# Gates of the second expert layer: one of four parts kept in the staging buffer, the rest read back four slots at a time

## The reference

```python
idx = jnp.take_along_axis(cidx, pos, axis=-1)
g = jax.nn.softmax(top, axis=-1).astype(h.dtype)
...
def block(args):
    hx, ix, gx = args
    act = jax.nn.gelu(jnp.einsum('td,tkd->tk', hx, u_tab[ix]))
    return jnp.einsum('tk,tkd->td', gx * act, v_tab[ix])
```

## Time and profile before

| | us |
|---|---|
| median of 3 runs | 2998.86 |
| lowest and highest | 2987.83, 3002.03 |
| profiled execution | 3011.89 |
| its span, first to last instruction | 3010.1 |
| its slot loop, first to last `apply` of the second layer | 2241.6 to 2971.1 |

### The profile page before, as it was taken

The page is one execution under the profiler, slowest core; times in us unless marked ns, Lnnn a source line. Parts: engine busy times, 40 slices in busy tenths (PEclk is TensorE's granted clock), DMA queues, the critical chain, the costliest instruction groups (busy, mean ns, idle before and its releaser), DMA issues. The chain is left out here.

```text
span 3010.1 us, 44098 instructions
## 1 busy us (share of the span) xinstructions
PE 2578.7 (86%) x16181; PEld 2269.8 (75%) x16181; DVE 2375.5 (79%) x4626; ACT 1204.6 (40%) x1806; POOL 678.8 (23%) x486
## 2 busy tenths in 40 slices
PE   7976897789999889999879797897779999999765
PEld 4964797788998778887658677796678888888544
DVE  8876689985658999998883565489978888888886
ACT  3344343663333333333334223443654444444322
POOL 0000152111110112213320000152323443434552
PEclk9987899899999999999998898898989999999997
DMA  5720343687678889988861323144889999999995
GB/s 214 280 70 36 122 136 124 240 290 256 231 241 300 301 301 304 315 303 257 270 225 43 127 98 118 54 138 146 297 313 353 358 348 341 349 333 351 323 328 179
DMA packets 333353, 708.38 MB, mean 235 GB/s; under 512 B 172848, under 2 KB 175696, under 8 KB 326368
## 3 DMA queue, kind: packets, MB, share of 16 engines
q1 hardware_dynamic: 272896, 466.60, 45.5%
q0 software_dynamic: 55360, 201.38, 18.5%
q10 hardware_dynamic: 4896, 37.75, 3.1%
HBM read 640.89 MB, written 64.72 MB: 234 GB/s over the span
## 5 line engine op out<-in xcount | busy, mean ns | idle before, releaser
L1998 PE MATMUL pe_s<-hl_hi,pq_uh 128*128 128x320 f32 (+2 forms) x2304 | 719.2, 312 | 47.8 <-DVE pq_ul L163 26.2
L1999 PE MATMUL pe_s<-hl_lo,pq_uh 128*128 128x320 f32 (+2 forms) x2304 | 707.7, 307 | 0.0
L2000 PE MATMUL pe_s<-hl_hi,pq_ul 128*128 128x320 f32 (+2 forms) x2304 | 706.6, 307 | 0.0
L2081 PE MATMUL peer_acc<-val_vh,val_w 128*128 128x512 f32 x2048 | 612.4, 401 | 85.7 <-DVE val_w L163 85.6
L2081 PEld LDWEIGHTS peer_acc<-val_vh,val_w 128*128 128x128 f32 x2048 | 385.1, 193 | 182.3 <-DVE val_vl L163 104.4
L1998 PEld LDWEIGHTS pe_s<-hl_hi,pq_uh 128*128 128x128 f32 x2304 | 452.2, 196 | 70.6 <-issue 37.7
L1999 PEld LDWEIGHTS pe_s<-hl_lo,pq_uh 128*128 128x128 f32 x2304 | 452.6, 196 | 8.4
L2000 PEld LDWEIGHTS pe_s<-hl_hi,pq_ul 128*128 128x128 f32 x2304 | 451.4, 196 | 0.0
L2255 POOL DMA_INDIRECT pe_frow<-in_peer_v,pe_fidx x192 | 317.6, 1654 | 557.4 <-DVE pe_fh L2431 239.4
L2255 POOL DMA_INDIRECT pe_frow<-in_peer_rows,pe_fidx x192 | 236.5, 1232 | 838.5 <-DVE pe_frow L2415 775.1
L163 DVE TENSOR_TENSOR val_vl<-val_vr,val_vh 128x1024 fp32r<-128x1024 f32 x256 | 312.4, 1220 | 108.7 <-ACT val_vh L2199 107.9
(11 more groups left out here) (489 smaller groups left out, 4010.9 us busy)
## 6 DMA issues: line engine op xcount, KB each, us to landing
pq_ur<-in_peer_u SPq DMA_DIRECT2D x256, 512.0 KB
val_vr<-in_peer_v SPq DMA_DIRECT2D x256, 512.0 KB
gates<-gate_stg ACTq DMA_DIRECT2D x30, 1024.0 KB, 8.0
val_mrow<-in_ada_rows SPq DMA_DIRECT2D x56, 512.0 KB
val_gr<-gates SPq DMA_DIRECT2D x128, 160.0 KB, 4.9
pq_ur<-in_w_query SPq DMA_DIRECT2D x32, 512.0 KB, 7.8
s_wv<-val_out SPq DMA_DIRECT2D x32, 512.0 KB
val_gr<-gates SPq DMA_DIRECT2D x128, 128.0 KB
```

The lines of the kernel that those rows point to most:

```text
L1998: pe.matmul(o, r32(uh[:, b, k]), r32(hi[:, k, a:T]), start=k == 0, stop=False)
L1999: pe.matmul(o, r32(uh[:, b, k]), r32(lo[:, k, a:T]), start=False, stop=False)
L2000: mm = pe.matmul(o, r32(ul[:, b, k]), r32(hi[:, k, a:T]), start=False, stop=k == KC - 1)
L2081: mm = pe.matmul(acc[:, 2 * t + c, :], r32(lhs[:, b, w]), r32(rhs[:, b, c * 512:(c + 1) * 512]), start=False, stop=False, skip_group_check ...
```

## The change

`Plan` gets two more numbers: how many of the parts stay in the staging buffer (`held`) and how many slots one gate load covers (`each`). The first layer has 0 and 1, which is what it did; the second has 1 and 4.

```diff
+        self.held, self.each = held, each
+        self.stored = self.parts - held
+        self.odd_stored = (self.parts + 1) // 2 - held
...
-PLANS = Plan(64, [3] * 12 + [2] * 2), Plan(128, [2] * 16)
+PLANS = Plan(64, [3] * 12 + [2] * 2, 0, 1), Plan(128, [2] * 16, 1, 4)
...
-        gr = x.sb("gr", [P, 2, PARTS, HALF])
+        gr = x.sb("gr", [P, 2, plan.stored, EACH * HALF])
...
-            def gate(n, b):
-                src = gates_dram[0:PARTS, :, bass.ds(n, 1), :]
-                sp.dma_start(gr[:, b], src.rearrange("h p a c -> p h (a c)")).then_inc(gload[b], 16)
+            def gate(m):
+                src = gates_dram[0:plan.stored, :, m * EACH:(m + 1) * EACH, :]
+                sp.dma_start(gr[:, m % 2], src.rearrange("h p a c -> p h (a c)")).then_inc(gload[m % 2], 16)
...
                 if n == RING:
-                    sp.wait_ge(gst1, 16 * ((PARTS + 1) // 2))
-                    gate(0, 0)
-                    gate(1, 1)
+                    sp.wait_ge(gst1, 16 * plan.odd_stored)
+                    if plan.held:
+                        sp.wait_ge(gst2, 16 * (PIECES - 1) * plan.odd_stored)
+                    gate(0)
+                    gate(1)
...
-                    sp.wait_ge(applied, z.n + 1)
...
-                    gate(z.n + 2, b)
+                    if (z.n + 1) % EACH == 0 and z.n + 1 + EACH < NB:
+                        sp.wait_ge(applied, z.n + 1)
...
+                        gate((z.n + 1) // EACH + 1)
...
-                if c >= full:
+                if full <= c < plan.stored * (full + 1) + full:
                     store_piece(c, (c - full) // (full + 1), (c - full) % (full + 1))
...
-            act.wait_ge(evacd, CHUNKS)
-            store_rest(PARTS - 1, SOON, SOON + REST)
+            if not plan.held:
+                act.wait_ge(evacd, CHUNKS)
+                store_rest(PARTS - 1, SOON, SOON + REST)
...
             def apply(z, ahead):
-                b = (z.n + ahead) % 2
-                dve.wait_ge(gload[b], z.turn(ahead) * 16 + 16)
-                dve.wait_ge(drained, z.n + (ahead + J + 3))
-                a = A[:, z.place(ahead)]
-                v.tensor_tensor(a, a, gr[:, b].rearrange("p h c -> p (h c)"), ALU.mult).then_inc(applied, 1)
+                n = z.n + ahead
+                m, at = n // EACH, n % EACH * HALF
+                dve.wait_ge(gload[m % 2], m // 2 * 16 + 16)
+                dve.wait_ge(drained, n + (J + 3))
+                a = A[:, z.place(ahead), 0:held].rearrange("p (h c) -> p h c", c=HALF)
+                ins = v.tensor_tensor(a, a, gr[:, m % 2, :, at:at + HALF], ALU.mult)
+                if plan.held:
+                    a = A[:, z.place(ahead), held:TOKENS]
+                    ins = v.tensor_tensor(a, a, stg[:, 1, n], ALU.mult)
+                ins.then_inc(applied, 1)
```

More of the change, by code:

```diff
@@ L1685, with __init__ @@
 class Plan:
-    def __init__(self, fetched, groups):
+    def __init__(self, fetched, groups, held, each):
         self.fetched = self.first = fetched
@@ L1854, in mix_experts @@
     RING, LAST, SPANS, CHUNKS, PARTS = plan.ring, plan.last, plan.spans, plan.chunks, plan.parts
-    FROM, TOKENS = plan.first, plan.tokens
+    FROM, TOKENS, EACH = plan.first, plan.tokens, plan.each
+    held = plan.stored * HALF
     flat = s.sb("A", [P, RING * TOKENS])
@@ L1888, in mix_experts @@
         else:
-            x.sb("kept", [P, 2 * NKEYS * HALF - 6 * D - 2 * TOKENS])
+            x.sb("kept", [P, 2 * NKEYS * HALF - 6 * D - 2 * plan.stored * EACH * HALF])
         pair = x.sb("w", [P, 2, 2 * TOKENS])
@@ L1960, in slot @@
                     value(z.n + 2, b)
-                    sp.wait_ge(applied, z.n + 1)
-                    if z.n + 2 >= SOON:
-                        sp.wait_ge(gst2, 16 * ((PIECES - 1) * ((PARTS + 1) // 2 - 1) + 2))
-                    gate(z.n + 2, b)
+                    if (z.n + 1) % EACH == 0 and z.n + 1 + EACH < NB:
+                        sp.wait_ge(applied, z.n + 1)
+                        if z.n + 2 >= SOON and not plan.held:
+                            sp.wait_ge(gst2, 16 * ((PIECES - 1) * (plan.odd_stored - 1) + 2))
+                        gate((z.n + 1) // EACH + 1)
                 if layer == 0:
@@ L2227, in slot @@
                 expert_gelu(LAST + z.n)
-                if z.n == 0:
+                if z.n == 0 and not plan.held:
                     store_rest(PARTS - 1, SOON + REST, NKEYS)
```

## The result

The changed kernel takes 2980.3 us (median of 13 runs) against 2999.0 of 13 runs of the kernel before on the same chip: ratio 0.9939, 95% interval 0.9925 to 0.9953, 18.6 us less. The forecast of 2962, 37 us less, had the sign, and about twice the size of the first measurement.

What follows compares the result with a forecast made beforehand. PE and the DMA engines were taken as both almost full in the middle, with DVE waiting for gates. Middle 19, tail 12 and entry 8 less 2 for DVE made 37 us, giving 2962 us; range 2938 to 2990.

Steps and rivals of the forecast that it cites:

- Entry: Start of the second layer's slot loop, 2226 to 2304 us: 8 us gained (3 to 12), mainly from stores leaving the holes.
- hole of 9 us: At the entry, DVE waits 9.2 us for slot 2's gates; moving 3 MB of stores out was to return 5.1 us.
- Middle: 80 second-layer slots, 2304 to 2788 us: 19 us gained (8 to 26) from earlier gate loads and freed DMA time.
- the values take the place of the gates: Rival for middle and tail: values land as late as gates did, only 5 us there, 2988 us in all; chance 0.12.
- The full engines: Middle: DMA engines 97% busy, 5.87 us a slot, taken as almost full; 0.25 us a slot freed, to 5.62.
- packet prices: DMA engine time for each packet: 17 ns for 256 bytes, 50 for 1 KB, 176 for 4 KB.
- PE's floor: Middle: PE needs 5.75 us of each 6.05 us slot, so it can return at most its waiting time.
- Tail: 37 last slots without products, 2793 to 2971 us: 12 us gained (5 to 25), less 2 for DVE's split `apply`.
- the sign that I had named for packets and not bytes alone: Tail: with the DMA share unchanged, GB/s staying at 325 means only bytes counted; rising GB/s means packets did.
- The second instruction's price: DVE's `apply` split into 192 and 64 columns: 74 ns a slot with overlap, 2 us lost in the tail (0 to 6).
- Only bytes count: Rival for the whole loop: memory is full, not the engines' packets; 17 us gained, 2982 us; chance 0.16.
- Slower: Rival for the loop: DVE's added instruction and bursts of gate loads cost more than the entry gains; 3032 us; chance 0.06.

Runs made afterwards that it cites:

- e1: The changed kernel, but gates loaded for one slot at a time, the last part still held in the staging buffer; 2977.3 us, ratio 0.9909.
- e4: The changed kernel, but the last part is also stored to DRAM as before (4 MB in three DMAs), which nobody reads; 2988.5 us, ratio 0.9941.
- e2: The kernel before with gates loaded for four slots at a time, all four parts stored in DRAM; 2997.3 us, ratio 0.9975.
- e3: The changed kernel with SP's order in a second-layer slot turned: value block, gates, then table block; 2944.0 us, ratio 0.9795.
- e6: The kernel before with only SP's second-layer order turned (value block, gates, then table block); 2968.8 us, ratio 0.986.
- e7: The changed kernel with gates loaded one slot at a time and SP's second-layer order turned (values, gates, table block); 2950.5 us, ratio 0.981.
- e9: The same kernel as e3, run again on another chip; 2941.5 us, ratio 0.980 to the kernel before.
- e10: The same kernel as e9 with two more unused DVE multiplications in each second-layer slot; 2948.6 us, ratio 0.9816.

## Why the prediction was wrong

**Entry: size too small, cause half right.** I had 8 us (3 to 12); it gained 12.9 and 12.7. I had the hole of 9 us right and the stores as its cause, which e1 bears out: without them alone the entry takes 25.1 us. But I made the sum from the stores' bytes, and left out the second way: e4 and e2 show that asking for the gates of slot 2 with the first load removes the hole even with the stores there. I had counted PE's idle time in the holes (12.6 us) and subtracted 1.3 for larger first loads; nearly all came back, at the entry's marks.

**Middle: the step that failed.** I had 19 us (8 to 26); it gave 0.1 in one profile and lost 3.6 in the other. The rival "the values take the place of the gates", with 0.12, is what happened in the middle; its 5 us for middle and tail together were too few, because the tail gained. The failing step was reading one row of a wait, 2.1 of 3.9 us, as what a slot would gain, as if the values would then be there. They weren't: SP asked for them 1.9 us after their buffer was free (median of the middle, before and after; 0.03 us in e3 and e6) and behind 512 KB of table, and PE's wait for `val_w` stayed at 23.1 us for 23.6, where I had it below 10. e3 and e6 show that this was the cause: with the values asked for first, PE's wait is gone (not among the waits of e3's middle, 1.1 us in e6's) and a slot takes 5.62 us, with the change and without it. The prediction said that the values' wait is "hidden now" and priced its return at half; it came back at 74.1 of 76.3 us. Why it came back whole and not in part is not shown beyond that; that queues as full as before delay the next block by as much as DVE had won is my reading.

**The full engines: a wrong reading of the share.** I took 97% DMA share as a resource that paces the loop and counted 0.25 us a slot of freed time towards it. Share fell as forecast (5.87 to 0.93 x 6.02 = 5.60 us a slot, where I had 5.62), and nothing moved. e6 settles it: in the turned order the same kernel with the same small packets moves 374 GB/s in 5.62 us slots. The packet prices were right: taken packet by packet from the traces, one of 256 bytes takes 18.0 ns in the middle before and one of 1 KB 52.3 in the middle after (median 46), for my 17 and 50. They were only not what anybody waited for in the middle.

**PE's floor: too high.** I took 5.75 us a slot from busy time. e3, e6, e7 and e9 all run at 5.62. Busy time for each matmul record fell by 2.3% from the middle before to that of e3 (159.5 to 155.8 ns). The granted clock, 0.99 and 1.00, accounts for about 1% of it; the rest is open (the ends of matmuls are modelled in the profile).

**Tail: the size right, the cause in part open.** I had 12 less 2; it gained 12.7 and 9.3 in 36 slots. The rate rose from 325 to 338 GB/s at the same share of 0.94, the sign that I had named for packets and not bytes alone. e1 (a quarter fewer packets and bytes, at the old distance) and e2 (the same bytes in larger packets, asked for further ahead) each have most of it (4.55 and 4.51 for 4.82), which is less than additive. No run has larger packets without the distance, so these two aren't parted. DVE, 90% busy then, is the likely next limit. The second instruction's price of 0 to 6 us holds by the times (e10: 3 to 4); its pair starts 0.27 us apart, for my 0.28.

**The rivals.** "Only bytes count" with the limit of the memory is refuted for the middle by 374 GB/s over 460 us. DMA: Bandwidth & Descriptors in the Trainium skill (Where 436 GB/s comes from) has about 358 GB/s for the memory, as the share of each of two cores. The same section speaks of 425 GB/s measured, and this case, on one core, agrees with that in so far as it passed 358. That rival's total, 2982, is nearest to the 2980.3 measured, but by luck: its parts are 8 in the middle (0 came), 3 in the tail (9 to 13) and 6 net at the entry (13). "Slower" did not come.

**The range** held the time, 2938 to 2990, because it had been drawn to reach the rivals. With nothing from the middle, the sum of the other terms as I had them is 12 + 8 - 2 = 18 us, the 18.6 measured; that too is partly luck, as the entry alone gave 5 more than its term.

## What to carry to other kernels

When a wait for one of two blocks that are loaded side by side is removed, look at when the other is asked for, and behind what: in this double-buffered loop the later one took over 74 of 76 us of waiting, and gave them back only when it was asked for earlier too. Read the issue queue in order: each wait in it delays everything behind it, so loads should stand in the order in which their buffers come free, and the block that is needed first should be ahead in the queue. A DMA share of 97% isn't yet a bound: compare the stretch with one in which the consumer never waits, before giving freed time a price.

## What the runs showed of the hardware

The DMA engines of the one core that this kernel runs on moved 374 GB/s through 460 us, with the DMA share of the profile at 1.02, while 512 packets of 256 bytes went with every 1920 KB of large ones (e6). A packet of 256 bytes took 18.0 ns of an engine on average, one of 1 KB 52.3, one of 4 KB 172 to 177 (middle before and after). A DVE operation of 0.22 us starts 0.27 us after the start of the one before it, which takes 0.35. And a hole can need two causes at once: the entry's hole went with either of two edits, and their gains of 10 and 14 us don't add.
